# Expert weights in fixed places by parity: w1 in two, w2 in one, loops over two experts, and TensorE's first expert steps reordered

## The reference

```
h = RMSNorm(x)
logits = h @ w_router + b_router          # 32 experts, the top 4 for each token
gates  = softmax(top 4 logits)
for each expert e and its tokens:
    gu   = h @ w1[e] + b1[e]              # 1024 -> 2048
    gate = min(gu[:, :1024], 7);  up = clip(gu[:, 1024:], -7, 7)
    y    = ((up + 1) * gate * sigmoid(1.702 * gate)) @ w2[e] + b2[e]   # 1024 -> 1024
    out[token] += gates[token, e] * y
out = RMSNorm(x + out) * norm_final_g
```

## Time and profile before

| | |
|---|---|
| median of 3 runs | 1227.8 us (1227.31 to 1229.17) |
| the profiled execution | 1227.92 us |
| its span | 1225.9 us |
| TensorE matmul busy | 1169.0 us (95%) |
| VectorE, ScalarE, GpSimd busy | 428.0, 207.7, 58.5 us |
| mean granted TensorE clock | 0.999 |
| moved by DMA | 461.79 MB, mean 377 GB/s |

### The profile page before, as it was taken

The page is one execution under the profiler, slowest core; times in us unless marked ns, Lnnn a source line. Parts: engine busy times, 40 slices in busy tenths (PEclk is TensorE's granted clock), DMA queues, the critical chain, the costliest instruction groups (busy, mean ns, idle before and its releaser), DMA issues.

```text
span 1225.9 us, 17199 instructions
## 1 busy us (share of the span) xinstructions
PE 1169.0 (95%) x7154; PEld 588.0 (48%) x7154; DVE 428.0 (35%) x741; ACT 207.7 (17%) x306; POOL 58.5 (5%) x43
## 2 busy tenths in 40 slices
PE   9999999999999999999999999999999899999897
PEld 8888888888643334333333333333333333333332
DVE  5886764655632223222222222222222222222222
ACT  6444553534400000000000000000000000000001
POOL 0850000000300000000000000000000000000000
PEclk9999999999999999999999999999999999999999
DMA  9756437877889999999999999999999999999996
GB/s 310 272 207 217 161 138 258 317 283 320 337 350 428 431 433 433 429 431 434 433 430 430 433 433 432 429 433 434 432 429 433 433 433 428 433 433 434 428 423 255
DMA packets 47522, 461.79 MB, mean 377 GB/s; under 512 B 4985, under 2 KB 6978, under 8 KB 32290
## 3 DMA queue, kind: packets, MB, share of 16 engines
q1 hardware_dynamic: 44760, 458.97, 89.9%
q10 hardware_dynamic: 2730, 2.36, 0.7%
HBM read 459.19 MB, written 1.07 MB: 375 GB/s over the span
## 4 chain that ended last, share of the span: by engine, by line
PE 66%; DMA 32%; DVE 1%; SPq 1%; ACT 0%; issue 0%; DVEq 0%; ACTq 0%
PE ps L1289 19%; DMA w_ring<-in_w 19%; PE ps L1355 12%; DMA A_QK<-in_w 6%; DMA xb_and_att<-in_w 6%; PE ps L1006 4%; PE ps L1444 4%; PE ps L1014 3%; PE ps L1012 3%; PE ps L1013 3%; PE ps L1263 2%; PE ps L1007 2%; PE ps L1026 1%; PE ps L1139 1%; PE ps L1141 1%; PE ps L1140 1%
## 5 line engine op out<-in xcount | busy, mean ns | idle before, releaser
L1289 PE MATMUL ps<-w_ring,A_W 128*64 128x512 f32 x1216 | 272.5, 596 | 28.9 <-DMA w_ring<-in_w 28.4
L1890 DVE TENSOR_SCALAR A_W<-ps 128x512 f32<-128x512 f32 x32 | 22.1, 692 | 478.2 <-PE ps L1289 478.2
L1289 PEld LDWEIGHTS ps<-w_ring,A_W 128*64 128x64 f32 x1216 | 84.8, 137 | 200.9 <-issue 160.2
L1355 PE MATMUL ps<-w_ring,A_W 128*64 128x512 f32 x608 | 137.9, 595 | 0.0
L1534 DVE TENSOR_TENSOR w_parts<-w_ring,w_parts 128x1024 fp32r<-128x1024 f32 x76 | 109.9, 1463 | 56.4 <-ACT w_parts L733 55.5
L1289 PE MATMUL ps<-A_QK,A_W 128*64 128x512 f32 x416 | 93.2, 595 | 9.3 <-DMA A_QK<-in_w 9.3
L918 ACT ACTIVATE A_W<-ps 128x512 f32<-128x512 f32 x31 | 18.5, 597 | 462.9 <-PE ps L1336 462.9
L1289 PE MATMUL ps<-xb_and_att,A_W 128*64 128x512 f32 x384 | 86.2, 596 | 9.4 <-DMA xb_and_att<-in_w 9.4
L733 ACT ACTIVATE w_parts<-w_ring 128x1024 fp32r<-128x1024 f32 x75 | 78.9, 1058 | 64.6 <-PE ps L1007 32.1
L914 ACT ACTIVATE A_W<-A_W 128x512 f32<-128x512 f32 x32 | 20.2, 631 | 359.8 <-DVE A_W L1890 359.8
L1006 PE MATMUL ps<-hT_both,w_parts 128*128 128x512 f32 x224 | 79.3, 399 | 0.0
(11 more groups left out here) (266 smaller groups left out, 1198.7 us busy)
## 6 DMA issues: line engine op xcount, KB each, us to landing
w_ring<-in_w SPq DMA_DIRECT2D x110, 2048.0 KB, 35.2
A_QK<-in_w SPq DMA_DIRECT2D x38, 2048.0 KB, 35.1
xb_and_att<-in_w SPq DMA_DIRECT2D x35, 2048.0 KB, 35.2
w_ring<-in_w_in SPq DMA_DIRECT2D x36, 1024.0 KB, 7.3
w_ring<-in_w SPq DMA_DIRECT2D x8, 1024.0 KB, 23.7
w_ring<-in_w_ret_branch SPq DMA_DIRECT2D x2, 2048.0 KB, 10.9
xb_and_att<-in_w SPq DMA_DIRECT2D x4, 1024.0 KB, 20.6
A_W<-in_w_out SPq DMA_DIRECT2D x1, 2560.0 KB, 13.0
```

The source lines that it names most:

```text
L1289: mm = pe.matmul(o, XT[:, k, :], hidden_columns(tile[:, j, :], c), start=(k == 0), stop=(k == KC - 1))
L1355: mm = pe.matmul(ps[CAP * c:CAP * c + CAP, 3, :], lhs, w2_tile(flat)[:, q % W2_ROWS, c * HALF:(c + 1) * HALF], start=False, stop=(q == FQ ...
L1890: dve.tensor_scalar(gl, bank(0), LIMIT, None, ALU.min).then_inc(s.g, 1)
```

## The change

There is no ring any more. w1 of even experts lies in w1_ring, w1 of odd ones in w1_odd (xb, A_ATT and A_QK, which lie side by side), w2 in w2_ring. A_W[0:4096] (LATE_UNIT) serves as an eleventh place for two units: w2 (1, 0) and then w2 (2, 1). w2 of 31 goes to w1_ring. A w1 load waits until the same unit of expert e - 2 has been passed; a w2 pair waits until w2 of expert e - 1 has been passed. In the loop the order of loads is: first pair of w1 of k + 2, w2 of k, second pair of w1 of k + 2. The first experts' loads are written out, and so are four experts on TensorE; loops then run over TURN = 2 experts.

```
-RING = 10
-TURN = 5
+TURN = 2
+        w1_places = [w1_flat, w1_odd[:, :]]
+        LATE_UNIT = A_W[:, 0:UNIT_WORDS]
+        LAST_W2 = ((N_EXP - 2, 0), (N_EXP - 2, 1), (N_EXP - 1, 0))
+        def w2_place(e, u):
+            if (e, u) in ((1, 0), (2, 1)):
+                return LATE_UNIT
+            if (e, u) == (1, 1):
+                return w2_part(0)
+            if (e, u) == (2, 0):
+                return w2_part(1)
+            return w1_part(u) if e == N_EXP - 1 else w2_part(u)
+        def load_w1_units(sp, e, units):
+            for u in units:
+                sp.wait_ge(s_used, w1_number(e - 2, u) + 1)
+                load_w1(sp, e, u)
+        def load_w1_pair(sp, e, k, u, used):
+            to = w1_places[k % 2][:, u * UNIT_WORDS:(u + 2) * UNIT_WORDS].rearrange("p (j n) -> p j n", j=PAIR_ROWS)
+            source = w1_both(e, u)
+            sp.wait_ge(s_used, used + w1_number(k - 2, u + 1) + 1)
+            for odd in range(2):
+                sp.dma_start(to[odd::2], source[odd::2]).then_inc(s_w1[k % 2][u // 2], 16)
+        def load_w2_pair(sp, e, k, used):
+            to, source = w2_flat.rearrange("p (j n) -> p j n", j=FQ), w2_both(e)
+            sp.wait_ge(s_used, used + w2_number(k - 1, 1) + 1)
+            for odd in range(2):
+                sp.dma_start(to[odd::2], source[odd::2]).then_inc(s_w2, 16)
```

SP's loads before the stage keep their waits and take other contents; then:

```
             sp.wait_ge(s_wl, LAST_UNIT + 6)
-            load_w1(sp, 1, 0, 4)
+            load_w2(sp, 0, 0)
             sp.wait_ge(s_wl, LAST_UNIT + 8)
-            load_first(sp, 0)
+            load_w1(sp, 1, 1)
             sp.wait_ge(s_wl, LAST_BRANCH)
-            load_w1(sp, 1, 1, 5)
+            load_w2(sp, 0, 1)
...
             sp.wait_ge(s_wl, LAST_BRANCH + 4)
+            load_w2(sp, 1, 0)
+            sp.wait_ge(s_wu, LAST_BRANCH + UNITS)
             load_first(sp, 3)
-            sp.wait_ge(s_wu, LAST_BRANCH + UNITS)
-            load_w2(sp, 0, 1, 9)
             sp.wait_ge(s_wo, 3)
-            load_w2(sp, 0, 0, 8)
+            load_first(sp, 2)
             sp.wait_ge(s_x2, 2 * TT)
-            load_w1(sp, 2, 0, 10)
-            for u in range(HALF_UNITS):
+            load_w1(sp, 1, 0)
+            for u in range(W1_UNITS):
...
+            load_w1_units(sp, 3, range(W1_UNITS))
+            sp.wait_ge(s_used, w2_number(0, 0) + 1)
+            load_w2(sp, 1, 1)
+            sp.wait_ge(s_used, w2_number(0, 1) + 1)
+            load_w2(sp, 2, 0)
+            load_w1_units(sp, 4, range(W1_UNITS))
+            sp.wait_ge(s_used, w2_number(1, 0) + 1)
+            load_w2(sp, 2, 1)
+            sp.wait_ge(s_used, w2_number(1, 1) + 1)
+            load_w2(sp, 3, 0)
+            load_w1_units(sp, 5, (0, 1))
+            sp.wait_ge(s_used, w2_number(2, 0) + 1)
+            load_w2(sp, 3, 1)
+            load_w1_units(sp, 5, (2, 3))
+            with sp.Fori(0, (N_EXP - 8) // TURN) as r:
+                for k in range(4, 4 + TURN):
+                    used = r * (TURN * E_UNITS)
+                    load_w1_pair(sp, r * TURN + k + 2, k + 2, 0, used)
+                    load_w2_pair(sp, r * TURN + k, k, used)
+                    load_w1_pair(sp, r * TURN + k + 2, k + 2, 2, used)
+            load_w1_pair(sp, N_EXP - 2, N_EXP - 2, 0, 0)
+            load_w2_pair(sp, N_EXP - 4, N_EXP - 4, 0)
+            load_w1_pair(sp, N_EXP - 2, N_EXP - 2, 2, 0)
+            load_w2_pair(sp, N_EXP - 3, N_EXP - 3, 0)
```

The final gain is no longer spread by TensorE. SP loads it to all partitions behind the last w2 quarter:

```
+            sp.wait_ge(s_lo, 2 * TT)
+            sp.dma_start(gain[:, :], bass.AP(g_final.tensor, 0, [[0, P], [1, D]])).then_inc(s_gain, 16)
```

```
-                    hidden_unit(first_units[u], u, s_wu if u < HALF_UNITS else None).then_inc(s_used, 1)
+                    hidden_unit(w1_place(0, u), u, s_wu, FIRST_BANK, XT_first).then_inc(s_used, 1)
                     if u == 2:
-                        hidden_bias(main, 0)
+                        hidden_bias(main, 0, FIRST_BANK)
                         second_scales()
-                        spread_gain()
+                        pe.wait_ge(s_lo, 2 * TT)
+                        gather(main, 1, scaled=True)
...
             hidden_first()
-            pe.wait_ge(s_lo, 2 * TT)
-            gather(main, 1, scaled=True)
-            pe.wait_ge(main.scales, 2)
-            fill(3, 8)
-            pe.wait_ge(s_res, 2 * TT)
...
+            for k in range(4):
+                expert(k, k, 0)
+            with pe.Fori(0, (N_EXP - 6) // TURN) as r:
+                for k in range(4, 4 + TURN):
+                    expert(r * TURN + k, k, r)
```

More of the change, by code:

```diff
@@ L462, in load_expert_w2, with w1_place @@
[L462 to L473, removed]
+        def w1_place(e, u):
+            return w1_places[e % 2][:, u * UNIT_WORDS:(u + 1) * UNIT_WORDS]
@@ L598, in _ @@
-            for i in range(1, TURN):
-                load_expert_w1(sp, i + 1, i + 1, 0)
-                load_expert_w2(sp, i, i, 0)
-            with sp.Fori(1, (N_EXP - 2) // TURN) as r:
-                for i in range(TURN):
-                    load_expert_w1(sp, r * TURN + i + 1, TURN + i + 1, (r - 1) * (TURN * E_UNITS))
-                    load_expert_w2(sp, r * TURN + i, TURN + i, (r - 1) * (TURN * E_UNITS))
-            for u in range(W1_UNITS):
-                n = w1_number(N_EXP - 1, u)
-                sp.wait_ge(s_used, n - RING + 1)
-                sp.dma_start(w1_tile(place(n)[0]), w1_source(N_EXP - 1, u)).then_inc(s_unit[u], 16)
@@ L902, in _, with store_residual @@
                                accum_out=gden[:, t:t + 1]).then_inc(s_tke, 1)
-            for t in range(TT):
-                if t:
-                    act.wait_ge(s_gainp, 1)
-                    act.wait_ge(s_lo, 2 * TT)
-                    act.activation(gain[:, :], bank(6, 2), ACT.Copy).then_inc(s_gain, 1)
-                    act.wait_ge(s_gain, 1)
+            def store_residual(t):
                 for h in range(2):
@@ L1363, in down_unit, with project_down @@
                 return mm
-            def project_down(i, first, rounds=0):
+            def project_down(i, k, more):
                 down_bias(main, i)
                 for u in range(W2_UNITS):
-                    flat, landed, count = place(first + u)
-                    pe.wait_ge(landed, 2 * rounds + count)
-                    down_unit(flat, u).then_inc(s_used, 1)
+                    landed, count = w2_landed(k, u)
+                    pe.wait_ge(landed, more + count)
+                    down_unit(w2_place(k, u), u).then_inc(s_used, 1)
                     if u == 0:
@@ L1390, in down_halves @@
             def down_halves(n, e, u, row):
-                flat = place(w2_number(e, u))[0]
+                flat = w2_place(e, u)
                 for h in range(2):
@@ L1465, in second_scales @@
                 gather_scales().then_inc(main.gathered, 1)
-            def spread_gain():
-                pe.wait_ge(s_grows, 32)
-                for c in range(KC):
-                    mm = pe.matmul(psf[:, 6 * HALF + c * P:6 * HALF + (c + 1) * P],
-                                   ident[0:KC, c:c + 1].broadcast_to([KC, P]), g_rows[:, :], start=(c % 4 == 0),
-                                   stop=True, skip_group_check=True)
-                mm.then_inc(s_gainp, 1)
             fill(0, 6)
@@ L1479, in _, with expert, transpose_previous @@
             hidden_first()
[L1480 to L1500 removed]
+            def expert(i, k, round_number):
+                def transpose_previous():
+                    pe.wait_ge(main.swe, i + 1)
+                    transpose_act(main, i)
+                hidden(i + 1, k + 1, round_number * (16 * TURN), transpose_previous)
+                pe.wait_ge(main.ate, i + 1)
+                pe.wait_ge(main.ye, i + 1)
+                gather(main, i + 2)
+                scatter(main, i)
+                pe.wait_ge(main.x, i + 3)
+                project_down(i, k, round_number * (32 * TURN))
+            for k in range(4):
[3 more added lines that the diff above has]
+                    expert(r * TURN + k, k, r)
             pe.wait_ge(s_table, 1)
```

147 lines of the change are left out of this document (63 added, 84 removed).

## The result

The changed kernel takes **1233.9 us**, median of 5 runs (1233.75 to 1234.19), against 1229.1 us for the kernel before in the same comparison (1227.31 to 1229.17). The ratio is 1.0044, 95% interval 1.0029 to 1.0059: slower. The profiled execution took 1233.9 us with a span of 1231.9 us, 6.0 us over the span before. The forecast was 1234.8 us, +7.0 us over 1227.8. By the medians of this comparison the difference is 4.8 us, by the profiled executions 6.0: the runs of the kernel before fall into two groups, near 1227.4 and near 1229.1 us, and its profile (1227.92) belongs to the first.

The account below looks back on a forecast made before the run. The queue of weight loads sets the loop's pace; behind its last wait TensorE binds the tail, without slack. Stream +1.3 and order +5.7 make +7.0 us over 1227.8: 1234.8 us, range 1228 to 1240.

Parts of the forecast that it names:

- The first steps: Start of the expert stage: gain spread, filler and wait gone, gather before unit 3; expert 1 starts at 336.33, 3.1 us earlier.
- The new hole: Early expert stage: queue empty from 437.0 to 442.5 us, 5.5 us, as w2 of 4 waits for its one place.
- The count of 19 units and four periods: w2 of 4: turn 19 units after 344.7, at 437.0 us; gate four TensorE periods after expert 1's start, at 441.4 us.
- The turn of w2 of 5: One expert after w2 of 4: its gate opens at 468.8 us, before its turn at 471.4, so it starves nothing.
- The stream term: Queue's delivery of weights after the restart at 442.5 us: 1.3 us later than in the kernel before.
- 441.2: Kernel before: time in us when the queue had delivered the same count of units, 34, as stand before w2 of 4.
- The order's lag: Loop and tail: w2 lands one pair later than its order of use; free in the middle, 5.7 us at the end.
- L + 5.7: Tail: TensorE reaches expert 30's second w1 pair 5.7 us after that pair's landing, L; before, it came there at L.
- The clock rival: Loop: single waits of 2.9 us before w2 might lower TensorE's granted clock, giving a slower time; chance 7%.
- signs of being wrong: In the profile after: no hole near 437, waits before w1 as before, expert 1 still at 339, or PEclk under 1.00.
- The gain's load: Tail: 0.5 MB load behind the last w2 quarter, 1.2 us of queue, expected hidden; uncovered it would cost 1.2 us.
- TURN: Loops over 2 experts instead of 5: no wait stands for a round's turn, so 0, at most tenths.

Follow-up runs that it names:

- Number 4: Changed kernel with 52 filler matmuls (about 3.1 us) behind the gather of expert 1, delaying TensorE's first steps: 1237.9 us, ratio 1.0078 to the kernel before.
- number 2: Changed kernel with w2 of 4 loaded behind both pairs of w1 of 6, the loop starting two experts later: 1230.6 us, ratio 1.0022 to the kernel before.
- 1: Changed kernel with, behind the loop, w2 of 28 loaded before the first pair of w1 of 30: 1231.2 us, ratio 1.0029 to the kernel before.
- 5: Changed kernel with w2 loaded before both pairs of w1 in the loop and behind it, one w2 place: 1238.1 us, ratio 1.0084 to the kernel before.
- 3: Changed kernel with both reorderings: w2 of 4 behind both pairs of w1 of 6, w2 of 28 before the first pair of w1 of 30: 1229.1 us, ratio 1.0009.
- 10: The changed kernel again, unedited, to check the spread between comparisons: 1235.6 us, ratio 1.0067 to the kernel before.
- number 9 without the loop: Kernel before with the change's first steps and TensorE's loop over 5 experts written out, without a jump: 1231.6 us, ratio 1.0033 to the kernel before.
- number 8: Kernel before with only the change's first steps, residual and gain; ring, load order and TURN = 5 stay: 1233.0 us, ratio 1.0037 to the kernel before.
- number 9: Three kernels on code position: kernel before minus 24 early fillers (1237.0 us); kernel before with the change's first steps, padded by 24 tiny matmuls (1224.3) or loop written out (1231.6).
- number 9, padded: Kernel before with the change's first steps, plus 24 tiny matmuls near 8 us restoring the 48 instructions: 1224.3 us, ratio 0.9972 to the kernel before.
- number 7: Changed kernel with both reorderings, each w2 unit also loaded behind its own gate with its own semaphore: 1224.7 us, ratio 0.9977 to the kernel before.

## Why the prediction was right

**The first steps.** Predicted 336.33 us for expert 1, measured 335.96. The gather took 1.49 us (1.41 in the sum) and unit 3 3.48 (3.59; 332.48 + 3.48 = 335.96); 0.26 us of the difference arose ahead of the stage, where expert 0 began sooner (319.89 instead of 320.15). Neither XT nor the activation made a wait.

**The new hole.** Predicted 437.0 to 442.5 us, 5.5 us; measured 437.0 to 442.26, 5.3 us. The count of 19 units and four periods held. TensorE had passed w2 of 3 at 440.95 us (441.4 in the sum), and from there the restart took 1.3 us where I had 1.15; from the issue it took 0.94. Number 4 shows that the hole follows TensorE, number 2 that it is this one gate. (The turn of w2 of 5 was summed wrongly: 442.5 plus six units is 471.6 and not 471.4. Nothing hangs on it.)

**The stream term** was the mis-sized one: +1.3 us predicted. w2 of 28 was there at 1154.51 us, so the second pair of expert 30 by count at 1154.51 + 9.71 = 1164.22, where the kernel before had 1164.36: -0.1. Of the 1.4 us, 0.24 is that the queue restarted at 442.26 and not at 442.5. About 0.65 is that the stream of before moved 429 GB/s and not 432 between 346 and 440 us, so that its "441.2" was really about 441.9. The other 0.5 us stays open.

**The order's lag.** Predicted L + 5.7; measured 1170.0 - 1164.22 = 5.8 us. The waits lie where the prediction put them, before w2 alone, and numbers 1 and 5 show that the order of the pairs makes them. Two details differ. They don't begin at expert 8 but at w2 of 6 (513.46 us, 0.98 us). And they are not 2.9 us each but in most of the loop 2.7 and 1.0 to 1.3 by turns: a long one lowers the clock, the 16 matmuls behind it take 5.1 to 5.4 us instead of 3.6, and the next wait is shorter by as much. Twice they took 6.6 to 6.7 us and the next wait was gone altogether, which is why there are 21 waits for 23 experts.

**The clock rival** was right that longer waits can bring the clock down: behind the wait before 542.60 the granted clock was 0.50 for 2.5 us. In the loop the next wait was shorter by what the slower matmuls took. One of the prediction's own signs of being wrong, PEclk under 1.00 after the waits, did come (0.52 and 0.63 behind the wait before 542.60), and the time was right all the same; as a sign it was badly chosen. To move the end, a lowered clock would have had to follow the last wait, which was a short one (0.97 us, matmuls at 3.65). Which of the two kinds the last wait would be was not forecast. It was a short one in numbers 1, 2, 3, 4 and 10 too (0.98 to 1.27 us), and by these rows a long one would have put about 1.7 us (5.35 - 3.65) on the end, so a part of the agreement is luck. The forecast's range up to 1240 takes in about half of a clock case whose size no run shows; what the runs of this kernel show behind a wait of 2.66 to 2.68 us is 16 matmuls in 5.06 to 6.67 us instead of 3.65, at most 3.0 us more. In the rows of the changed kernel, waits of 0.97 to 1.3 us left the clock at 1.00 and those of 2.66 to 2.68 us brought the lower level (0.50 in windows of 0.5 us behind the ones before 542.60 and 1125.38), while those of 2.59 us (659.16) and 2.56 us (1037.97) were followed by matmuls at 3.65. The length of the wait alone doesn't decide: in number 4 two waits of 2.67 us (545.27, 924.08) left the matmuls at 3.65, and in number 9 without the loop one of 2.11 us (687.23) was followed by 16 matmuls of 5.35 us. The prediction gives for a clock of 1.00; they list waits and no clock, and what shows it is the mean granted clock of 0.999.

**The gain's load and TURN.** The load is issued late in the tail and nothing waits for it. TURN was costed at 0, "none stands for the turn of a round". For this pair of kernels that is what the pages show: 24 and 25 packets of instructions, 0.2 us of "issue" in both. But the reasoning was thin. That the kernel before had no pause hung on where its loop of five experts began: numbers 8 and 9 show that the reordered first steps, with 48 instructions fewer ahead of that loop, would by themselves have cost 5.5 us of last matmul. The loop over two experts showed nothing of the kind in either of two positions, and the rows that the prediction used don't say so. The loop of five was moved in numbers 8 and 9. The loop of two was moved in number 4, where 52 matmuls more stand ahead of it: 26 packets in all, none between 500 and 1180 us, no pause. A loop of two inside the old ring was not tried. So leaving TURN out of the sum was right, but more by luck than by reasoning.

**The sum.** +7.0 predicted, +5.6 by the last matmul and +6.0 by the span. What is left of the change if its parts are set apart: the first steps are worth -4.0 us (number 9, padded), and the places and their order cost 1222.32 - 1212.75 = 9.6 us, of which the lag is 5.8 and the stream, 1164.22 against 1160.39, the other 3.8. From the other side, numbers 1 to 3 win back 5.9, and number 7, which also frees w2 by units, 8.4.

## What to carry to other kernels

When places are given to fixed owners, write down for each load at the head of the queue two times, its turn by count and its gate by the consumer's period; the one load whose gate is later makes the hole, and everything behind it is late by that (here number 2 made the hole 3.3 us shorter, and the last matmul came 3.4 us sooner). Then look at the order of the last loads against the order of use: in the steady loop a wrong order only moved the waits (from before w1 to before w2, with 29.14 us an expert in both kernels), but behind the last wait it was paid in full (5.8 us). And when an edit changes the number of instructions ahead of a large loop, read the instruction queue's packets and the "issue" waits first, before explaining the time by anything else.

## What the runs showed of the hardware

**A loop's place in the program can cost 0.7%.** 48 instructions fewer near 7 us, of no use to the result, took the kernel with TensorE's loop of five experts from 1227.7 to 1237.0 us (number 9, ratio 1.0074). Its instruction queue went from 24 packets (0.39 MB) to 69 (1.13 MB), about 16 KB each, and in the stretch from 500 to 1180 us from none to 41, nine of them from 612 to 754 and nine from 754 to 896 us. Behind each of the five jumps back TensorE paused twice, for 3.0 to 4.6 us (3.1 to 5.0 in number 8). The kernel before has the same jumps with neither a packet nor a pause there, and so has the padded kernel, but for one packet between 500 and 1180 us. What decides between the two cases is not shown: only two positions 48 instructions apart were tried for this loop.

**More packets of code went with a later stream of weights.** In the kernel without a loop TensorE never paused for its code, but with 34 packets more than in the padded kernel the second pair of expert 30 came 6.4 us later. That is about 0.2 us for each further packet on the mean, where 16 KB at the measured 432 GB/s would be 0.04. From 650 to 900 us the whole rate was 430 instead of 432 GB/s, which accounts for a part. The steps of number 9 say more: the six packets between 716.91 and 833.47 us went with 0.1 us, two before them and two behind with 1.5 us each time. How that arises was not settled.
